# Recurrent units of a hybrid trunk on one NeuronCore: inclusive sums on VectorE, the state decayed after its update, turns and modulation columns as transposes

## The reference, cut to what matters

```python
cum = jnp.cumsum(log_a, axis=3)
cum_last = cum[:, :, :, -1:, :]
q_t = q * jnp.exp(cum)
k_t = k * jnp.exp(-cum)
k_end = k * jnp.exp(cum_last - cum)
att = jnp.where(mask, jnp.einsum('bhncd,bhnsd->bhncs', q_t, k_t), 0.0)
u = jnp.einsum('bhnsd,bhnsv->bhndv', k_end, v)
decay = jnp.exp(cum_last[:, :, :, 0, :])
# state after a chunk: decay * s + u;  output: att @ v + q_t @ s
mod = silu(cond) @ w_mod[li] + b_mod[li]     # 6 * 1024 columns
```

## Time and profile before

| | us |
|---|---|
| median of 3 timed runs | 1445.62 |
| lowest, highest | 1437.51, 1451.51 |
| the profiled execution | 1439.02 |
| its span in the profile | 1437.2 |

### The profile page before, as it was taken

One profiled execution on the slowest core, in us unless ns is written; L12 is line 12 of the kernel. 1 busy time (PEld: TensorE's weight loads), 2 busy tenths in 40 slices (PEclk: granted clock), 3 DMA queues, 4 the chain that ended last, 5 costly groups with the idle time before them and its releaser, 6 DMA issues.

```text
span 1437.2 us, 38565 instructions
## 1 busy us (share of the span) xinstructions
PE 1272.3 (89%) x16808; PEld 892.2 (62%) x16808; DVE 521.0 (36%) x1111; ACT 334.6 (23%) x665; POOL 168.0 (12%) x228
## 2 busy tenths in 40 slices
PE   5989999989999898999989749987699899999882
PEld 2448854458888746787777524445464577877651
DVE  1324444135546764311111133446665351111113
ACT  2323221133332213100000032433562221000001
POOL 2004310013434000000000012010000000000001
PEclk8999999999999998999999969999899899999996
DMA  9941148361111127799999975116264379999995
GB/s 391 346 165 62 62 166 271 146 210 51 61 62 62 59 104 305 267 395 391 405 405 414 425 300 182 60 65 234 76 228 176 131 246 385 392 410 404 415 425 176
DMA packets 40230, 342.40 MB, mean 238 GB/s; under 512 B 6474, under 2 KB 11546, under 8 KB 21792
## 3 DMA queue, kind: packets, MB, share of 16 engines
q1 hardware_dynamic: 21888, 302.11, 53.1%
q0 software_dynamic: 7104, 19.57, 4.2%
q10 hardware_dynamic: 11104, 18.75, 4.1%
HBM read 322.30 MB, written 21.45 MB: 239 GB/s over the span
## 4 chain that ended last, share of the span: by engine, by line
PE 69%; DMA 15%; DVE 7%; issue 6%; ACT 2%; ACTq 0%; POOLq 0%; SPq 0%; POOL 0%; DVEq 0%
PE PB L739 64%; DMA arena<-in_w_moe 7%; PE PB L742 5%; DMA ring<-in_w_moe 4%; DVE arena L2091 3%; DMA ring<-in_w_mix 2%; ACT arena L1609 1%; DVE small L2104 1%; DMA ring<-in_w_mod 1%; DMA arena<-expert_out,rows_i 1%; DMA expert_out<-arena 1%; DVE arena L2098 1%; DVE x L2091 1%; DVE arena L2095 0%; DVE arena L2101 0%
## 5 line engine op out<-in xcount | busy, mean ns | idle before, releaser
L739 PE MATMUL PB<-arena 64*64 64x64 f32 (+6 forms) x9476 | 456.6, 290 | 32.0 <-DMA arena<-in_w_moe 12.2
L739 PEld LDWEIGHTS PB<-arena 64*64 64x64 f32 (+3 forms) x9476 | 360.6, 129 | 124.0 <-issue 43.3
L739 PE MATMUL PB<-ring,hT 128*128 128x512 f32 (+1 forms) x720 | 313.5, 591 | 8.4 <-DVE hT L2094 3.6
L739 PEld LDWEIGHTS PB<-ring,hT 128*128 128x128 f32 x720 | 136.8, 193 | 167.6 <-issue 161.6
L739 PE MATMUL PB<-ring,arena 128*32 128x256 f32 (+2 forms) x3520 | 201.7, 385 | 18.3 <-DMA ring<-in_w_moe 18.3
L739 PEld LDWEIGHTS PB<-ring,arena 128*32 128x32 f32 x3520 | 164.2, 111 | 51.5 <-issue 28.0
L1609 ACT ACTIVATE arena<-PB 128x256 f32<-128x256 f32 (+3 forms) x209 | 102.6, 491 | 319.4 <-PE PB L739 272.4
L742 PE MATMUL PB<-cst,arena 128*128 128x128 f32 (+2 forms) x734 | 106.9, 289 | 39.4 <-DVE arena L2091 17.2
L742 PEld LDWEIGHTS PB<-cst,arena 128*128 128x128 f32 (+2 forms) x734 | 84.4, 151 | 76.2 <-issue 41.1
L2512 DVE TENSOR_TENSOR arena<-arena,PB 128x256 f32<-128x256 f32 (+1 forms) x32 | 15.1, 471 | 265.9 <-PE PB L739 148.9
L589 POOL TENSOR_TENSOR arena<-arena,cst 128x256 f32<-128x256 f32 x72 | 49.3, 702 | 263.9 <-DVE arena L2091 245.2
(11 more groups left out here) (152 smaller groups left out, 923.7 us busy)
## 6 DMA issues: line engine op xcount, KB each, us to landing
arena<-in_w_moe SPq DMA_DIRECT2D x50, 2048.0 KB, 21.5
ring<-in_w_moe SPq DMA_DIRECT2D x44, 2048.0 KB, 22.2
ring<-in_w_mod SPq DMA_DIRECT2D x24, 2048.0 KB, 8.5
ring<-in_w_mix SPq DMA_DIRECT2D x22, 2048.0 KB, 8.6
expert_out<-gate ACTq DMA_DIRECT2D x1, 3456.0 KB, 21.7
expert_out<-arena ACTq DMA_DIRECT2D x12, 288.0 KB
tokens<-arena ACTq DMA_DIRECT2D x6, 512.0 KB, 3.3
hT<-in_w_moe SPq DMA_DIRECT2D x2, 1536.0 KB, 8.6
```

The source lines that it names most:

```text
L739: return nc.tensor.matmul(out, lhsT, rhs, start=start, stop=stop, **k)
```

## The change

- `gla_sums`: TensorE's second product (the rest of the sum) goes, with ScalarE's third exponential and GpSimd's third product.
- `gla_add` multiplies k_t (`tg` 1) in place of k_end. The state takes it in first (VectorE, in place in `SG`, "gsum"), and then GpSimd decays it in place ("gS"); both steps stand behind GpSimd's level work.
- `gla_turn`: four 128x128 transposes replace sixteen 64x64 products; ScalarE copies them out in four parts of 64 partitions.
- `prep` part 1: the inclusive product on TensorE goes; VectorE makes it as exclusive sum + the token's own value into `sums` (SBUF), ahead of level 4's subtractions, and ScalarE waits for it before both exponentials.
- `mod_columns`: four transposes replace four products with `fold`; VectorE's `mod_chunk` adds the four strips with a reduction before the bias.

```diff
@@ pool
-                mul(tg[:, 2, :], tg[:, 2, :], E[:, i, EK_:EK_ + 256], "gend", g, n)
-
-            def gla_kept(g, n, d, step):
+
+            def gla_decayed(g, n, d, step):
 
                 c = (step, 1 - step)[d]
-                if step:
-                    pool.wait_ge(*when("gS", g, n, 0))
-                else:
-                    pool.wait_ge(*when("g_dec", g, n))
-                    if n:
-                        pool.wait_ge(*when("gS", g, n - 1, 1))
+                pool.wait_ge(*when("g_dec", g, n))
+                pool.wait_ge(*when("gsum", g, n, step))
                 dec = small[:, 16:24].rearrange("p (h c) -> p h c", c=2)[:, :, c]
-                mul(kept, SG[:, d, :, :], bc(dec, 2, 128), "kept", g, n, step)
+                mul(SG[:, d, :, :], SG[:, d, :, :], bc(dec, 2, 128), "gS", g, n, step)
...
-                        if v == 3:
-                            gla_kept(g, n, d, 0)
...
-                    gla_kept(g, n, d, 1)
+                    gla_decayed(g, n, d, 0)
+                    gla_decayed(g, n, d, 1)
@@ tensor
-                    ins = mm(PB[:, bank, at + 2 * j:at + 2 * j + 2], mrow[:, b, 128 * j:128 * j + 128], C("fold"))
+                    ins = tp(PB[:, bank, 128 * j:128 * j + 128], mrow[:, b, 128 * j:128 * j + 128])
...
-                mm(PB[:, 7, 0:256], inc, la)
-                mm(PB[:, 7, 256:512], rest, la).then_inc(*tick("pe", "gcum", g, n))
+                mm(PB[:, 7, 0:256], inc, la).then_inc(*tick("pe", "gcum", g, n))
...
-                    for h in range(4):
-                        ins = both(lambda c, r: mm(PB[r, 7, 256 * a + 64 * h:256 * a + 64 * h + 64], tg[r, a, 64 * h:64 * h + 64],
-                                                   ident[r, r]))
+                    for j in range(2):
+                        ins = tp(PB[:, 7, 256 * a + 128 * j:256 * a + 128 * j + 128], tg[:, a, 128 * j:128 * j + 128])
...
-                if step == 0:
-                    pe.wait_ge(*when("gend", g, n))
-                claim(7, "gS", g, n, step)
+                claim(7, "gsum", g, n, step)
                 for h in range(4):
                     for e in range(2):
-                        ins = mm(PB[64 * e:64 * e + 64, 7, 128 * h:128 * h + 128], tg[r, 2, 64 * h:64 * h + 64],
+                        ins = mm(PB[64 * e:64 * e + 64, 7, 128 * h:128 * h + 128], tg[r, 1, 64 * h:64 * h + 64],
...
                 if step == 0:
+                    if n:
+                        pe.wait_ge(*when("gS", g, n - 1, 1))
                     pe.wait_ge(*when("gatt", g, n))
...
-                claim(banks[1], "e_dec", *u)
-                mm(PB[:, banks[1], :], inc, lw).then_inc(*tick("pe", "sum_inc", *u))
@@ scalar
-                fn(tg[:, 1, :], PB[:, 7, 0:256], ACT.Exp, scale=-s)
-                fn(tg[:, 2, :], PB[:, 7, 256:512], ACT.Exp, "g_exp", g, n, scale=s)
+                fn(tg[:, 1, :], PB[:, 7, 0:256], ACT.Exp, "g_exp", g, n, scale=-s)
...
-                fn(GT.rearrange("p a h n -> p (a h n)"), PB[:, 7, :], ACT.Copy, "GT", g, n)
+                for c in range(2):
+                    for e in range(2):
+                        fn(GT[64 * c:64 * c + 64, :, e:4:2, :],
+                           PB[64 * e:64 * e + 64, 7, :].rearrange("p (a j c n) -> p c a j n", a=2, j=2, c=2)[:, c, :, :, :],
+                           ACT.Copy, *(("GT", g, n) if c and e else ()))
...
-                    act.wait_ge(*when("sum_exc", *u))
+                    act.wait_ge(*when("sums", *u))
...
-                    act.wait_ge(*when("sum_inc", *u))
-                    fn(k[:, 1, :], PB[:, banks[1], :], ACT.Exp, "e_inc", *u, scale=-RW / 2, bias=C("bias", 3 * d + 2, 1))
+                    fn(k[:, 1, :], sums, ACT.Exp, "e_inc", *u, scale=-RW / 2, bias=C("bias", 3 * d + 2, 1))
@@ vector
                 dve.wait_ge(*when("modp", l, n))
-                tt(modTv[:, l, 4 * n:4 * n + 4, :], PB[:, bank, at:at + 8].rearrange("p (j c) -> p j c", c=2),
-                   bc(cols[:, COL_BM + 48 * l + 4 * n:COL_BM + 48 * l + 4 * n + 4], 2, 2), ALU.add, "modT", l, n)
+                red(col, PB[:, bank, :].rearrange("p (j s c) -> p j c s", j=4, s=4)[:, :, 0:2, :])
+                tt(col, col, bc(cols[:, COL_BM + 48 * l + 4 * n:COL_BM + 48 * l + 4 * n + 4], 2, 2), ALU.add, "modT", l, n)
...
-                dve.wait_ge(*when("kept", g, n, step))
                 dve.wait_ge(*when("gu", g, n, step))
...
-                tt(SG[:, d, :, :], kept, PB[:, 7, :].rearrange("p (h n) -> p h n", h=4), ALU.add, "gS", g, n, step)
+                dve.wait_ge(*when("gr", g, n, step))
+                tt(SG[:, d, :, :], SG[:, d, :, :], PB[:, 7, :].rearrange("p (h n) -> p h n", h=4), ALU.add, "gsum", g, n, step)
...
+                elif part == "sums":
+                    dve.wait_ge(*when("sum_exc", *u))
+                    tt(sums, PB[:, banks[0], :], tmpE[0], ALU.add, "sums", *u)
...
                     if v == 4:
                         gla_att(g, n)
+                        if not last:
+                            prep(g, n + 1, "sums")
...
                     if n == 5:
+                        prep(g, 0, "sums", (4, 5))
                         prep(g, 0, 4)
```

More of the change, by code:

```diff
@@ L47 @@
 _at = 0
-for _n, _w in [("ident", 128), ("fold", 2), ("one", 1), ("half", 2), ("eye", 64), ("bias", 8), ("tie", 16),
+for _n, _w in [("ident", 128), ("one", 1), ("half", 2), ("eye", 64), ("bias", 8), ("tie", 16),
                ("lt", 128), ("le", 128), ("gt", 128), ("ge", 128),
@@ L231, in build @@
         g2w = gate[:, 2 * D:2 * D + 512]
+        sums = gate[:, 2 * D + 512:3 * D]
         stg = G4[:, 0, :].rearrange("p (h n) -> p h n", h=8)
@@ L654, in _ @@
             meet(pool, "pool", "units0")
+            pool.wait_ge(*when("gS", 0, len(units[0]) - 1, 1))
             for d in range(2):
@@ L903, in gla_sums @@
                 i, d = units[g][n]
-                inc, rest = (C("le"), C("gt")) if d == 0 else (C("ge"), C("lt"))
+                inc = C("le") if d == 0 else C("ge")
                 la = LA[:, i, 256 * d:256 * d + 256]
@@ L978, in prep @@
                 u = (g, n)
-                inc, exc = (C("le"), C("lt")) if d == 0 else (C("ge"), C("gt"))
+                exc = C("lt") if d == 0 else C("gt")
                 if part == 0:
@@ L1771, in totals @@
                 if n:
-                    act.wait_ge(*when("kept", g, n - 1, 1))
+                    act.wait_ge(*when("gS", g, n - 1, 1))
                 fn(small[:, 16:24], PB[:, 1, 0:8], ACT.Exp, "g_dec", g, n, scale=1.0 / 16)
@@ L1799, in prep @@
                     fn(k[:, 0, :], PB[:, banks[0], :], ACT.Exp, "e_exc", *u, scale=-RW / 2, bias=C("bias", 3 * d, 1))
-                    act.wait_ge(*when("sum_inc", *u))
-                    fn(k[:, 1, :], PB[:, banks[1], :], ACT.Exp, "e_inc", *u, scale=-RW / 2, bias=C("bias", 3 * d + 2, 1))
+                    fn(k[:, 1, :], sums, ACT.Exp, "e_inc", *u, scale=-RW / 2, bias=C("bias", 3 * d + 2, 1))
                 else:
                     act.wait_ge(*when("rates", *u))
-                    fn(tmpE[1], PB[:, banks[1], :], ACT.Exp, "e_dec", *u, scale=RW / 2, bias=C("bias", 3 * d + 1, 1))
+                    fn(tmpE[1], sums, ACT.Exp, "e_dec", *u, scale=RW / 2, bias=C("bias", 3 * d + 1, 1))
             def turns(g, n):
@@ L2199, in gla_state @@
                 d = units[g][n][1]
-                dve.wait_ge(*when("kept", g, n, step))
                 dve.wait_ge(*when("gu", g, n, step))
-                if step:
-                    dve.wait_ge(*when("gr", g, n, 1))
-                else:
-                    dve.wait_ge(*when("gr", g, n, 0))
-                tt(SG[:, d, :, :], kept, PB[:, 7, :].rearrange("p (h n) -> p h n", h=4), ALU.add, "gS", g, n, step)
+                dve.wait_ge(*when("gr", g, n, step))
+                tt(SG[:, d, :, :], SG[:, d, :, :], PB[:, 7, :].rearrange("p (h n) -> p h n", h=4), ALU.add, "gsum", g, n, step)
             def gla_out(g, n):
@@ L2211, in gla_out, with prep @@
                 tt(oG[:, i, :], oG[:, i, :], PB[:, 6, :], ALU.add, "gout", g, n)
-            def prep(g, n, part):
+            def prep(g, n, part, banks=(2, 3)):
                 i, d = units[g][n]
@@ L2931, in constants @@
     put("one", 1.0)
-    put("fold", np.arange(P)[:, None] % 32 == np.arange(2)[None, :])
     m = np.zeros((P, NMOE), np.float32)
```

12 lines of the change are left out of this document (5 added, 7 removed).

## The result

| | before | after |
|---|---|---|
| median, runs side by side | 1443.09 (13 runs) | 1433.23 (13 runs) |
| lowest, highest | 1437.51, 1453.12 | 1427.66, 1437.01 |
| profiled execution, its span | 1439.02, 1437.2 | 1436.87, 1435.0 |

The ratio is 0.9929, with an interval of [0.991, 0.9948]: 10 us faster, within the 1% that the prediction called "same". The time predicted was 1428.0, the range 1417 to 1441. The range holds it, but the forecast's own sum was 15.8 us, and a third of it did not arrive. The prediction gave slightly more weight (0.48 to 0.46) to a gain beyond 1%, and that did not come.

What follows compares the result with a forecast made beforehand. TensorE bounds the recurrent units, the weight stream the experts. Savings of 10.6 (units), 3.0 (projections) and 2.2 (attention) sum to 15.8 us, off a typical 1443.4: 1427.6, rounded to 1428; range 1417 to 1441.

Steps and rivals of the forecast that it cites:

- 2.14 a full unit: Each unit that prepares a next one: 0.53 + 0.50 + 0.45 + 0.96 - 0.3 us saved; four give 8.6.
- Four prices: TensorE's costs in a unit: one gate sum 0.53, columns 0.48, turn 0.48, one 512-column decay sum 0.96 us.
- VectorE's sum and GpSimd's decay were covered: In units, VectorE's inclusive sum has 0.8 us of cover and GpSimd's state decay 2.2, so neither costs time.
- 2.2, as foreseen: Attention's eight modulation chunks: 1.5 us for five among the pairs, 0.7 for the first three; bounds 0 and 4.
- The four chunks at the start count nothing: Modulation chunks at the start gain nothing, since the projection waits 1.18 us for its weights at 47.98 all the same.
- rival 3: Slower: waits for the copies drop TensorE's clock in every unit; 30 us lost at 10 us each, 1458; chance 0.05.
- There the turn's gain goes and so does the copies' cost: Latents' last unit: TensorE waits for VectorE, so the turn and copies drop out; 0.53 + 0.50 - 0.2 = 0.8 us saved.
- the reduction, put at 0.2: VectorE's added 32-element reduction in each modulation chunk costs 0.2 us with its gap; it counts in the latents' last unit.
- Rival 1: Small operations are dear (copies 0.60, reductions 0.69, VectorE's sum late): gain 8 us, 1435; chance 0.15.
- Rival 2: The experts' weight stream swallows the gain; only attention's 2 us would be left, 1441; chance 0.06.
- the 14 us sooner: Sign of the forecast: loads of the experts' weights come some 14 us sooner.
- Rival 4: State's decay comes late on GpSimd, up to 1 us in each unit beyond its 2.2 cover: 1434; chance 0.06.

Runs made afterwards that it cites:

- again: The changed kernel unaltered, timed and profiled a second time: 1430.14, ratio 0.9921 against before.
- turns: Kernel before with only the turns of q and k changed, to four transposes and four copies: 1443.62, ratio 1.0004.
- inclusive: Kernel before with only the inclusive sum of the decays moved to VectorE: 1435.62, ratio 0.9943.
- state: Kernel before with only the state's path changed (no second gate sum, GpSimd decays the state after VectorE's sum): 1441.54, ratio 0.9978.
- experiment 3: Changed kernel with idle 512-column identity products added on TensorE in four waits: 1429.84, ratio 0.9928 against before.
- last_swap: Changed kernel with the latents' last unit's turn as before, and step 1's gla_add behind the next part's sixteen products in each unit: 1431.66, ratio 0.9887.
- best: last_swap plus idle products at the start and ahead of each group's first turns, the latents' ones ahead of TensorE's wait: 1423.78, ratio 0.9848 against before.
- last_turn: Changed kernel with only the latents' last unit's turn as before (sixteen products, one copy): 1432.03, ratio 0.9905 against before.

## Why the prediction was right, and where not

**The units.** 2.14 a full unit was foreseen; the four took 1.9 less on the mean in after and 2.2 in "again". Four prices were 0.1 too low (columns and turn 0.58 to 0.59 for 0.48), the copies' 0.2 too high (0.1 for 0.3). The mechanism holds: TensorE sets a full unit. VectorE's sum and GpSimd's decay were covered, as argued: the sum ended at 378.19 and its exponential started at 379.00, behind ScalarE's own copies.

**Projections and attention.** The latents' projection took 113.21 from its first product to the turns, before 115.25: 2.0 for 2.15. From the first of the loads of mixer weights into `ring` behind layer 0's experts (850.56 before, 847.86 after) to the end, the nine profiles with the columns as transposes have 586.3 on the mean, and the five without (before, turns, inclusive, state, before with idle products) 588.5: 2.2, as foreseen. Single ones spread by 5 (584.1 to 589.1 with, 586.5 to 590.4 without), so this is weak.

**"The four chunks at the start count nothing"** failed. I gave the edit no gain because the weights land all the same, and no loss either. But the time taken from TensorE ahead of a DMA is added to its wait, and the granted clock fell behind the longer wait: 3.4 us lost (with 0.9 foreseen from the inclusive sum). The row that I took as cover, 1.18 us of wait, was the warning. The longer wait explains the 2.3 us of the second chunk; the fall behind the unchanged wait of 2.75, which used up the inclusive sum's 0.9 and 0.85 more, it does not. That is rival 3's mechanism in another place: idle products in the wait kept the clock (experiment 3), so the wait has a part in it; that the transposes have none is not tested.

**"There the turn's gain goes and so does the copies' cost"**, for the latents' last unit, failed. I looked at VectorE, which TensorE waits for at 471.00, and not at ScalarE's queue, where the copies stand ahead of two table loads. Alone in the kernel before, the new turn came with a unit 2.5 us longer (the longer wait, the low clock behind it and a stall 0.5 longer); in the changed kernel with its turn as before the wait fell from 1.55 ("again") to 0.54. And the reduction, put at 0.2, was dearer there (experiment 3).

**Not foreseen at all:** the stalls of TensorE without a releaser, which edits of the code move. The price of the one in the last unit could not be told by times: 16 tiny products took it away and the median stayed.

**What is luck.** That the time fell within the range, though 6 us of the sum did not arrive, owes something to the range's width of 24 us. Where the medians lost these 6 us is not shown: the losses of the traces are in two executions of after, each slower than the median beside it.

**Rival 1** gave almost the time measured, for a reason that did not hold: in full units the small operations were cheap, and only in the last one dear. **Rival 2** falls: the first expert load is issued 2.62 sooner and layer 0's experts end 2.70 sooner (847.86 for 850.56), so the weight stream kept the gain made ahead of it; the 14 us sooner that the prediction named as a sign did not show in this pair. **Rival 4** falls: TensorE nowhere waits for GpSimd's decay.

## What to carry to other kernels

An edit ahead of a DMA wait is not worth nothing: it makes the wait longer, and what follows may run at half the clock. Idle products that fill such a wait, with the shift of code that they bring, gave some 8 us here by the medians (last_swap to best), and 3 (0 to 6) in the kernel before; where they stood behind the wait they took 5 us of TensorE. Price an edit in the odd unit (the last, the first) by the queues of that unit: an operation that is free in a full unit was paid in full where table loads stood behind it. And compare a stage in several profiles before you believe one, and set it beside its kernel's median: the code's place moves stalls of 1 to 2.5 us, and the pair compared first was 8 us further together than the medians.

## What the runs showed of the hardware that I had not expected

- A DMA queue named "instruction" moved packets of 16 KB, one for some 250 records of TensorE. During a 2 MB load TensorE stood still for 2.53 to 2.61 us with no releaser, in four executions (after, again, last_turn, last_swap) ahead of the same product; shifted by 16 products the stall was gone. That the two belong together is inferred.
- A granted clock of 0.50 followed such a stall (after) as it followed waits for DMA and for ScalarE: the same 64 products took 2.08 or 3.31 to 3.68. It did not follow each of them: 2.38 us of wait for ScalarE in after left it at 1.00, 1.61 in turns did not.
- A 128x8 addition on VectorE took 0.17 us with PSUM as a source (before, 462.38) and 0.73 from SBUF (the kernel with idle products, 453.09) in the same place of the last unit.
- Copies of 64 partitions by 256 took ScalarE 0.40 each, as much as 128 by 256 (0.40 at 464.87), so four cost 1.60 for the 0.60 of one full one.
